# A hybrid decoder step on one core: the samples' state products in seven parts between steps of the out-projection

## What is computed

```python
h = _rmsnorm(x, norm_mix)
z = h @ w_in                      # mixer A (gated short convolution), mixer B (gated DeltaNet, 4 heads x 128)
...
x = x + jnp.concatenate([y_a, y_b], axis=-1) @ w_out
x = x + _moe(_rmsnorm(x, norm_ffn), ...)      # top-1 of 4 groups, then top-2 of 8 experts
```

```python
# S_t = exp(g_t) (I - beta_t k_t k_t^T) S_{t-1} + beta_t k_t v_t^T ;  o_t = S_t^T q_t
```

## Time and profile before

| | |
|---|---|
| median of 3 runs | 1102.4 us (1100.69 to 1102.85) |
| profiled execution | 1102.69 us, span 1101.0 us |
| granted TensorE clock, mean of the span | 0.967 of full speed |
| TensorE busy | 94% of the span |
| VectorE, ScalarE, GpSimd busy | 43%, 32%, 8% |

### The profile page before, as it was taken

One profiled execution on the slowest core, in us unless ns is written; L12 is line 12 of the kernel. 1 busy time (PEld: TensorE's weight loads), 2 busy tenths in 40 slices (PEclk: granted clock), 3 DMA queues, 4 the chain that ended last, 5 costly groups with the idle time before them and its releaser, 6 DMA issues.

```text
span 1101.0 us, 16923 instructions
## 1 busy us (share of the span) xinstructions
PE 1036.5 (94%) x6688; PEld 920.2 (84%) x6688; DVE 472.0 (43%) x891; ACT 356.1 (32%) x767; POOL 88.0 (8%) x115
## 2 busy tenths in 40 slices
PE   5788999998999999999999979999999999999955
PEld 4678999998999999998888778888888888888722
DVE  5445677688344635466466582111111111111117
ACT  5456887332322322332222231121211212111115
POOL 2000000000000000000200030121121211211000
PEclk9889999998999999998899979999999999999978
DMA  6113566624663563566222188988888787898347
GB/s 225 26 39 101 123 152 150 175 92 139 194 185 104 154 169 105 148 205 185 72 77 78 43 312 323 359 315 327 307 319 317 295 321 303 324 343 295 134 181 312
DMA packets 118029, 220.94 MB, mean 201 GB/s; under 512 B 68428, under 2 KB 81286, under 8 KB 109262
## 3 DMA queue, kind: packets, MB, share of 16 engines
q1 hardware_dynamic: 105762, 194.20, 53.1%
q0 software_dynamic: 9792, 17.19, 4.2%
q10 hardware_dynamic: 2412, 8.68, 2.0%
HBM read 191.79 MB, written 46.72 MB: 217 GB/s over the span
## 4 chain that ended last, share of the span: by engine, by line
PE 87%; DVE 6%; ACT 3%; issue 2%; DMA 2%; SPq 0%; ACTq 0%; DVEq 0%; POOLq 0%
PE psum L1138 27%; PE psum L2169 22%; PE psum L2194 11%; PE psum L2039 9%; PE psum L2151 3%; PE psum L1161 1%; PE psum L1976 1%; PE psum L1478 1%; DVE it L951 1%; DVE xi L953 1%; DVE hl L848 1%; DMA y<-expert_rows 1%; PE psum L1243 1%; PE psum L1230 1%; PE psum L1236 1%
## 5 line engine op out<-in xcount | busy, mean ns | idle before, releaser
L1138 PE MATMUL psum<-hh,wh 128*128 128x350 f32 x672 | 226.9, 338 | 9.9 <-DVE hl L848 6.0
L1138 PE MATMUL psum<-hh,wl 128*128 128x350 f32 x672 | 221.0, 329 | 0.0
L1138 PE MATMUL psum<-hl,wh 128*128 128x350 f32 x672 | 220.5, 328 | 0.0
L1138 PEld LDWEIGHTS psum<-hh,wh 128*128 128x128 f32 x672 | 130.6, 194 | 12.0 <-issue 7.6
L2169 PE MATMUL psum<-xgt,wg 128*128 128x128 f32 x1088 | 130.0, 279 | 1.3 <-ACT xgt L2160 1.3
L1138 PEld LDWEIGHTS psum<-hl,wh 128*128 128x128 f32 x672 | 130.4, 194 | 0.9
L1138 PEld LDWEIGHTS psum<-hh,wl 128*128 128x128 f32 x672 | 129.9, 193 | 0.0
L2169 PEld LDWEIGHTS psum<-xgt,wg 128*128 128x128 f32 x1088 | 127.2, 196 | 1.9 <-issue 1.9
L2169 PE MATMUL psum<-xgt,wu 128*128 128x128 f32 x1088 | 127.0, 275 | 0.0
L2169 PEld LDWEIGHTS psum<-xgt,wu 128*128 128x128 f32 x1088 | 124.2, 192 | 0.0
L2181 DVE SCALAR_TENSOR_TENSOR ge<-thx,psum 128x256 f32<-128x256 f32 x34 | 14.3, 422 | 251.5 <-ACT thx L2175 251.5
(11 more groups left out here) (324 smaller groups left out, 1363.0 us busy)
## 6 DMA issues: line engine op xcount, KB each, us to landing
wg<-w_gate SPq DMA_DIRECT2D x34, 1024.0 KB, 5.0
wu<-w_up SPq DMA_DIRECT2D x34, 1024.0 KB, 8.7
wd<-w_down SPq DMA_DIRECT2D x34, 1024.0 KB, 11.3
wst<-w_in SPq DMA_DIRECT2D x28, 512.0 KB, 3.8
ck<-qkv_rows SPq DMA_DIRECT2D x9, 702.0 KB
qkv_rows<-acc SPq DMA_DIRECT2D x12, 520.0 KB, 6.1
xb<-x SPq DMA_DIRECT2D x8, 512.0 KB, 4.6
wo<-w_out SPq DMA_DIRECT2D x8, 512.0 KB, 6.9
```

Of the source, the lines that this page charges most:

```text
L1138: ins = mm(ps[:, c, 0:ZC], w[:, kk, :], a[:, kk, c * ZC:(c + 1) * ZC], start=(kk == 0 and q == 0), stop=(kk == KD - 1 and q == 2))
```

## The change

The products are issued in seven parts, the sum with all ones (L1479) in front of the first. Part `p` takes states `32p//7` to `32(p+1)//7`, so 4, 5, 4, 5, 4, 5 and 5 states, or 8 or 10 matmul instructions. Parts 0 to 4 stand ahead of steps 3 to 7 of tile 1, parts 5 and 6 ahead of steps 0 and 1 of tile 2. `pe2` is given by the last. On VectorE `second` moves from behind tile 1's x1 to behind its h2.

```diff
-    def products(pe):
-        pe.wait_ge(b.s_ok, NC)
-        pe.wait_ge(in_, 16)
-        pe.wait_ge(v, 8)
-        for k in range(SH):
-            mm(ps[:, 6, 2 * k:2 * k + 2], s_in[:, k, :], kq[:, k, :], start=True, stop=True)
-        mm(ps[:, 7, 0:SH], b.ones[:, :], flat(qk[:, :, :]), start=True, stop=True).then_inc(pe2, 1)
+    def products(pe, part):
+        if part == 0:
+            pe.wait_ge(b.s_ok, NC)
+            pe.wait_ge(in_, 16)
+            pe.wait_ge(v, 8)
+            mm(ps[:, 7, 0:SH], b.ones[:, :], flat(qk[:, :, :]), start=True, stop=True)
+        for k in range(SH * part // PRODUCT_PARTS, SH * (part + 1) // PRODUCT_PARTS):
+            ins = mm(ps[:, 6, 2 * k:2 * k + 2], s_in[:, k, :], kq[:, k, :], start=True, stop=True)
+        if part == PRODUCT_PARTS - 1:
+            ins.then_inc(pe2, 1)
...
+PRODUCT_PARTS = 7
...
-            if t == 1:
-                sample.second(dve)
             if t == 2:
                 sample.third(dve)
...
             stt(h2[t % 2][0:n, :], b.x1[0:n, t, :], b.stat[0:n, t, 2:3], wf[0:n, :], ALU.mult, ALU.mult
                 ).then_inc(h2_ok, 1)
+            if t == 1:
+                sample.second(dve)
...
-                if t == 1 and i == 6:
-                    sample.products(pe)
+                if t == 1 and i >= 3:
+                    sample.products(pe, i - 3)
+                if t == 2 and i <= 1:
+                    sample.products(pe, KD - 3 + i)
```

## The result

The changed kernel took 1091.47 us in the median of 4 runs (1090.36 to 1091.97), beside 1102.57 of the kernel before (1100.69 to 1102.85). The medians lie 11.1 us apart; the ratio on record is 0.9917, 95% interval 0.9893 to 0.9942: about 9.1 us less, 6.4 to 11.8. A second series of the same kernel gave 0.993 (0.9906 to 0.9954), 7.7 us.

What follows compares the result with a forecast made beforehand. The prediction took TensorE to bound the kernel, its clock halved under the products. Terms of -4.3, -0.2, -1.9, +0.5 and +0.1 gave -5.8 us, so 1097.0 us from 1102.7, range 1095.3 to 1111.0.

Steps and rivals of the forecast that it cites:

- What bounds it: From 499.81 to 557.28 us each piece of the chain is TensorE's; the clock falls under two-column matmuls without a gap.
- (a) to (c): Products at the high clock -4.3 us, sum with ones -0.2, out-projection steps behind -1.9, five more restarts +0.5.
- (d) the wait for `s_in`: The first part comes at 508.23 us, its load lands at 508.3: 0.1 us, bounds nothing and 1 to 2 us.
- (e) the update vectors: Made a step later on VectorE, ready 1.4 us before TensorE asks ahead of position(0): no cost.
- (f) GpSimd: Its scaling, 8.0 us of work from about 526 us, is wanted only after tile 8: no cost, even 15 us late.
- The rival of the fall: Clock falls under part 1 and the score, staying down until the last part is done: 1109.9 us; chance 0.41.
- the forecast: The clock stays up through the seven parts in the out-projection: 1097.0 us, by itself 1095.3 to 1098.5; chance 0.47.
- 1102.7 - 5.8: The profiled execution's time less the sum of the terms: 1096.9, say 1097.0 us, also the number for the median.

Runs made afterwards that it cites:

- 2.3 us of pad: The changed kernel with ten more matmuls of 512 columns at the first step of tile 1: 1101.71 us, its eight executions from 1093.89 to 1106.55.
- second_later_only: Against the kernel before, only the update vectors are made behind h2, the products staying one block: 1099.17 us, ratio 0.9983 (0.9965 to 1.0001).

## Why the prediction was right in its mechanism and wrong in its size

- *What bounds it*: right. All of the edited stretch is TensorE's in both profiles.
- *(a) to (c), products, steps behind, restarts*: right. Forecast -4.3 - 0.2 - 1.9 + 0.5 = -5.9 us, measured -6.4 from turn to turn, in two pairs of profiles. The pace at the high clock is 1.01/10 to 0.79/8, 0.10 us where I took 0.11, which over 64 gives the missing 0.5 us. Restarts of 0.1 us are there (1.49 against 1.39).
- *(d) the wait for `s_in`*: not there. In the changed kernel's profile the load was issued at 491.78 and took 13.4 us, to 505.2; the first product starts at 506.35. Forecast 0.1.
- *(e) the update vectors*: no wait of TensorE in the changed kernel; with the products as one block the same place costs a wait of 0.4 us ahead of position(0). With `second` left where it was, h2 and `choose` do stand behind the wait for the last part, as said, at a cost of 0.4 us.
- *(f) GpSimd*: right that its time isn't on the path (523.9 to 532.7 us), but its start had a price that I didn't see: too early it slows `choose(0)`.
- *The rival of the fall*: not the outcome, but real. With 2.3 us of pad four executions of eight are 11 us slower at a lower clock, and a longer part 1 or doubled products lose it in the profiled ones. Its condition was too strict: the clock can rise between parts. The rows couldn't tell it from the forecast (0.41 against 0.47), so it was in part luck that the clock held, and the pad shows how near it was.

The step that failed is the one that made a time out of the sum: "a microsecond that TensorE saves or loses there moves all that follows", and with it "1102.7 - 5.8", as if all else in the profiled execution would stay as it was. The sum has no term for what lies behind the out-projection, and that execution had a low stretch at the first expert too, worth 2.9 us. Of the 12.5 us between the first two profiles' spans, 6.4 are the edited stretch's, 2.9 the first expert's, 2.0 lie ahead of the edit and 1.2 elsewhere behind it. In the second pair (8.5 us) the 6.4 and the 2.9 are there again, and the out-projection starts 1.1 us later instead of 2.0 earlier. I allowed for such things only as "a low stretch elsewhere in the kernel that begins or ends differently shifts a run by about 1.7 us", to either side, and so ended the range at 1095.3.

What is shown: the seven parts aren't needed for the first expert's high clock, as it was there with the products still in one block (`second_later_only`), in two blocks, and in the kernel before with 0.7 or 2.7 us of more work at tile 4. What is argued from this, each time from one profile: that it depends on when the work behind tile 8 comes. What stays open: the low clock at this place is in both profiles of the kernel before and in none of the other fifteen, ten of which have the seven parts in some form or size, also with pads of 0.9 to 2.7 us; no run brought it on at will. Nor is it shown that this stretch is what parts the kernel before's two groups: they lie 5 us apart and it is worth 2.9, and with 2.7 us of pad the profiled one of three slow executions (1102.90 us) doesn't have it. Against the lower group, near 1097.5, the changed kernel's 1092 is 5.5 us better, close to the sum; against the upper one, near 1102.5, it is 10.5.

## What to carry to other kernels

A busy TensorE isn't one that keeps its clock: look at the granted clock under every block of matmuls with few columns, and price the block at the low clock together with the steps behind it. Cutting it in short parts between wide matmuls got that back here, but only with parts short also together with the small work already there: parts of 0.8 to 1.0 us held, parts of 1.6 to 2.0 and of 3.3 us didn't, nor did one of 2.7 us ahead of the score. The margin should be tried by shifting the stretch by some microseconds, and by more than one execution of each shift. Before a sum is taken from one profile, list its low stretches outside the edit and let the range include that each goes, at what it is worth (2.9 us here). A second profile alone wouldn't have warned: it had the same stretch. A longer series of times with their granted clocks would have: it falls in two groups, 5 us apart.

## What the runs showed that was not expected

With GpSimd's scaling beside them, some of VectorE's small instructions took 0.97 us instead of 0.19. Two blocks of 32 product instructions cost what one of 64 does, 27.5 us from turn to turn. One and the same kernel, the 2.3 us pad, ran in 1094 to 1099 us with a mean granted clock of 0.975 to 0.977, or in 1105 to 1107 with 0.967.
